# Depthwise convolution in token pairs through DRAM scratch, x loads on the scalar queue, and the gate of group B multiplied in another layout

## What is computed

```python
h = rmsnorm(x, norm_g) * (1.0 + scale[:, None, :]) + shift[:, None, :]
p = h @ w_in                                              # (B, L, 3584)
a_in, a_b, a_c, a_z, b_v, b_g, b_z = jnp.split(p, SPLITS, axis=-1)
y_a = a_b * dwconv(a_c * a_in, conv_a_w) * jax.nn.silu(a_z)          # 3 taps
u = b_v * jax.nn.sigmoid(b_g)
u = dwconv(u, conv_b_w) + conv_b_b                                   # 31 taps
y_b = jax.nn.silu(head_layernorm(u, ln_g, ln_b)) * jax.nn.silu(b_z)
y = jnp.concatenate([y_a, y_b], axis=-1) @ w_out
return x + gate[:, None, :] * y                           # then rmsnorm(., final_g)
```

## Time and profile before

| what | value |
|---|---|
| time, median of 3 runs | 2488.07 us (2486.75 to 2492.78) |
| the profiled execution's own time | 2490.17 us |
| its span, slowest core | 2488.6 us |
| spans of the 8 cores | 2471.5 to 2488.6 us |
| PE busy | 94% of the span |
| DVE, ACT, POOL busy | 47%, 42%, 21% |
| DMA | 142 GB/s on average |

### The profile page before, as it was taken

How to read it: one execution, slowest core, us unless ns; L and a number is a source line. 1 busy time by engine, 2 the same in 40 slices (tenths; PEclk the granted TensorE clock), 3 DMA queues, 4 the chain that set the end, 5 groups by cost and what they waited for, 6 DMA issues and landing times.

```text
span 2488.6 us, 42355 instructions; the slowest of 8 cores (2471.5 to 2488.6 us)
## 1 busy us (share of the span) xinstructions
PE 2330.9 (94%) x13702; PEld 1028.1 (41%) x13702; DVE 1163.8 (47%) x1859; ACT 1056.7 (42%) x1794; POOL 512.7 (21%) x620
## 2 busy tenths in 40 slices
PE   2899799999999999999999799997999979999797
PEld 0343344444444444444444344443444434444343
DVE  0241654445445544444554445454554554544547
ACT  0224444444544444345444245442454434454334
POOL 5112121122211111222121322122221122221203
PEclk9999899999999999999999899998999989999899
DMA  9944444455444445554444653436553445544444
GB/s 232 201 121 115 143 128 114 128 155 155 122 136 138 128 113 138 155 155 121 138 128 128 181 151 116 144 123 162 155 138 121 143 139 155 154 129 130 144 113 179
DMA packets 283012, 352.63 MB, mean 142 GB/s; under 512 B 152840, under 2 KB 225712, under 8 KB 281776
## 3 DMA queue, kind: packets, MB, share of 16 engines
q1 hardware_dynamic: 275184, 342.59, 48.4%
q0 software_dynamic: 7616, 7.34, 2.2%
HBM read 185.73 MB, written 67.13 MB: 102 GB/s over the span
## 4 chain that ended last, share of the span: by engine, by line
PE 86%; DMA 4%; DVE 3%; SPq 2%; issue 2%; POOL 1%; ACT 0%; DVEq 0%; POOLq 0%; ACTq 0%
PE pb L481 56%; PE pb L668 17%; PE pb L553 8%; DMA xb<-w_out 3%; PE pb L465 2%; PE pb L563 1%; SPq L329 1%; DVE tp L536 1%; PE pb L571 1%; DMA hraw<-xs 1%; POOL w_out_sb L447 1%; DMA yT<-w_ada 1%; SPq L292 0%; DVE tp L533 0%; DVE yT L539 0%
## 5 line engine op out<-in xcount | busy, mean ns | idle before, releaser
L481 PE MATMUL pb<-hT,w_in_sb 128*128 128x512 bf16 x6944 | 1507.2, 380 | 2.2 <-DVE hT L454 2.2
L481 PEld LDWEIGHTS pb<-hT,w_in_sb 128*128 128x128 bf16 x6944 | 680.1, 98 | 824.2 <-issue 7.2
L668 PE MATMUL pb<-w_out_sb,yT 128*128 128x512 bf16 x2048 | 460.6, 381 | 5.5 <-POOL yT L591 3.4
L553 PE MATMUL pb<-X,WC 128*32 128x512 bf16 x4096 | 248.5, 390 | 77.1 <-DVE ga L521 77.1
L668 PEld LDWEIGHTS pb<-w_out_sb,yT 128*128 128x128 bf16 x2048 | 199.6, 98 | 247.1 <-issue 19.0
L631 POOL TENSOR_TENSOR rsE<-msE,mhalf 128x1 f32<-128x1 f32 x128 | 70.2, 548 | 1111.5 <-DVE msE L629 1109.2
L513 DVE TENSOR_TENSOR t<-pb,tp 128x512 bf16<-128x512 f32 x128 | 88.9, 694 | 350.3 <-ACT xs L312 322.9
L519 ACT ACTIVATE tp<-pb 128x512 f32<-128x512 f32 x128 | 76.2, 597 | 412.1 <-DVE tp L536 142.7
L492 DVE SCALAR_TENSOR_TENSOR u<-tp,pb 128x512 bf16<-128x512 f32 x128 | 88.4, 691 | 279.5 <-PE pb L481 260.8
L581 DVE SCALAR_TENSOR_TENSOR pb<-pb,cbs,tp 128x512 f32<-128x512 f32 x128 | 96.8, 756 | 257.4 <-PE pb L571 193.8
L490 ACT ACTIVATE tp<-pb 128x512 f32<-128x512 f32 x128 | 76.1, 597 | 329.6 <-PE pb L481 272.1
(11 more groups left out here) (82 smaller groups left out, 1280.9 us busy)
## 6 DMA issues: line engine op xcount, KB each, us to landing
xb<-x SPq DMA_DIRECT2D x252, 512.0 KB, 6.7
X<-u SPq DMA_DIRECT2D x512, 135.0 KB, 2.9
y<-xb SPq DMA_DIRECT2D x124, 512.0 KB, 3.0
xb<-w_out SPq DMA_DIRECT2D x40, 512.0 KB, 8.2
w_in_sb<-w_in POOLq DMA_DIRECT2D x28, 256.0 KB, 22.1
yT<-w_ada SPq DMA_DIRECT2D x6, 1024.0 KB, 10.1
w_out_sb<-w_ada SPq DMA_DIRECT2D x6, 1024.0 KB, 14.8
xb<-gate_scratch SPq DMA_DIRECT2D x5, 512.0 KB, 6.4
```

The costliest lines, as they stand in the source:

```text
L481: T.op("tensor", lambda e, bank=bank, kc=kc: e.matmul(bank[:], lhsT=w_in_sb[:, kc, col0:col0 + 128], rhs=hT[:, kc, :], start=(kc == 0), st ...
L553: T.op("tensor", lambda e, q=q, g=g: e.matmul(bank[32 * g:32 * g + 32, :], lhsT=WC[:, j, g, q, :], rhs=X[:, j, g, 4 * q:4 * q + NT], start ...
L668: T.op("tensor", lambda e, bank=bank, kc=kc, sub=sub, h=h: e.matmul(bank[:], lhsT=yT[:, kc, sub * 128:(sub + 1) * 128], rhs=w_out_sb[:, kc ...
```

## The change

1. **Convolution in token pairs.** A tile's 512 columns are now its 256 odd tokens and then its 256 even tokens (`rows`). A partition of `X` is one of 8 shifts and one of 16 channels. A weight of 32 columns holds 16 channels for the even and the odd output, and one matmul covers 8 input tokens for 256 pairs. `NQ` falls from 8 to 4 and the groups of channels double: still 128 matmuls a tile, each 256 columns wide. The convolution's output has the parity of the token in the partition and both 64-channel halves side by side in the columns, so the norm's vectors (`cbs`, `lng`, `lnb`) differ between halves and several ACT and DVE steps are cut in two.
2. **X through DRAM.** `x_out` writes `u` to `u_scratch` (8 transfers, 544-byte runs), `x_in` reads it back (8 transfers of 16 partitions, 17 KB runs).
3. **The gate in the convolution's layout.** `g_out` and `g_in` bring `gb` through `g_scratch` into that layout, POOL multiplies there, `y_out` and `y_in` bring the product back into `yT`: 10 transfers a tile.
4. **Queues and places.** `a_load` and `d_loads` start on ACT's queue. `a_load` comes after `glu`, `a_square` moves from `t1_group` to `b2_b`, `a_scale` and `a_transpose` to behind `b2_b`, `d_loads` into `b2_a`. The halo copies go from POOL to DVE. All the `ln_*` steps run as hooks of `stage_d`, none between the `conv_b`.
5. **Fold.** `fold_gate` loads its first pieces during `glu`, uses `hraw` and one x buffer as staging, and does all 8 products on POOL.
6. **Start and end.** Tiles 0 and 1 are transposed by PE (`a_modulate`, i < 2) in place of the DMA; the last `stage_d` does the first four of its 8 accumulation steps for all 8 halves first.

```diff
@@ constants
-NQ = 8
-UW = NT + 32
-XW = NT + 4 * (NQ - 1)
+NQ = 4
+HN = NT // 2
+NG = 32
+PAD = 8
+UW = HN + 2 * PAD
+XN = NG * UW - 4
@@ a_load
-                T.dma("sync", lambda e, xbuf=xbuf, r=row0 + sub * 128: e.dma_start(out=xbuf[:], in_=x_d[r:r + 128, :]),
+                T.dma(eng, lambda e, xbuf=xbuf, sub=sub: e.dma_start(out=xbuf[:], in_=rows(x_d, i, sub)),
@@ fold_gate (new)
+            for kc in range(3):
+                load(kc)
+
+            def finish():
+                for kc in range(8):
+                    buf, keys = stg[kc % 3]
+                    T.op("gpsimd", lambda e, buf=buf, kc=kc: e.tensor_tensor(out=w_out_sb[:, kc, :], in0=buf, in1=gate_bc[:], op=ALU.mult),
+                         reads=keys + [gkey], writes=[("w_out", kc)])
+                    if kc + 3 < 8:
+                        load(kc + 3)
...
@@ transfers
-            fns = [lambda e, g=g, k4=k4: e.dma_start(out=X[32 * k4:32 * k4 + 32, :, g, :], in_=u[32 * g:32 * g + 32, :, k4:k4 + XW])
-                   for g in range(4) for k4 in range(4)]
-            T.dma_batch("sync", fns, [("u", slot)], ["X"], "xfill")
+        def x_out(i):
...
+            T.dma_batch("sync", [lambda e, h=h, j=j: e.dma_start(out=dst[h, j], in_=u_sb[i % 2][:, j, h, :]) for h in range(2) for j in range(4)],
+                        [("u", i % 2)], [("ud", i % 2)], "st_u")
...
+            T.dma_batch("sync", [lambda e, w=w: e.dma_start(out=Xf[16 * w:16 * w + 16, 0:XN], in_=ud[i % 2, w % 2, :, (w + 1) // 2:(w + 1) // 2 + XN])
+                                 for w in range(8)], [("ud", i % 2)], ["X"], "xfill")
@@ conv_b
-                        bank[32 * g:32 * g + 32, :], lhsT=WC[:, j, g, q, :], rhs=X[:, j, g, 4 * q:4 * q + NT],
+                            bank[32 * g:32 * g + 32, hh * HN:(hh + 1) * HN], lhsT=WC[:, G * NQ + q].rearrange("p c t -> p (c t)"),
+                            rhs=X[:, G, 4 * q:4 * q + HN], start=(hh == 0 and q == 0), stop=(hh == 1 and q == NQ - 1), tile_position=(0, 32 * g)),
@@ ln_out
-            T.op("gpsimd", lambda e: e.tensor_tensor(out=yT[:, 4 + j, :], in0=r[:], in1=gb[:, j, :], op=ALU.mult),
+            T.op("gpsimd", lambda e: e.tensor_tensor(out=yV[:, j, :], in0=r[:], in1=gbV[:, j, :], op=ALU.mult),
@@ conv_phase
+            cs = [conv_b(j) for j in range(4)]
...
+            return {0: norm((ln_center, 0), (ln_center, 1)),
+                    1: norm((ln_center, 2), (ln_var, 0), (ln_rstd, 0)),
+                    2: norm((ln_center, 3), (ln_var, 1), (ln_rstd, 1)),
+                    3: norm((ln_var, 2), (ln_rstd, 2)),
+                    4: norm((ln_var, 3), (ln_rstd, 3))}, (k, cs)
@@ main loop, behind glu
+            if 1 <= i < ntiles:
+                x_out(i - 1)
+            if left is not None:
+                y_out(i - 2)
+            if 1 <= i < ntiles:
+                x_in(i - 1)
+            if left is not None:
+                y_in(i - 2)
+            left = None
+            if 1 <= i <= ntiles:
+                g_in(i - 1)
+            if 1 <= i < ntiles - 1:
+                a_load(i + 1)
+            if 2 <= i and tile_first[i - 2]:
+                fold()
```

More of the change, by code:

```diff
@@ L539, in conv_a @@
[L539 to L547 removed]
+            out, okey = TP.next()
@@ L661, in stage_d, with half @@
             yT = yT2[i % 2]
-            row0 = i * NT
+            def half(sub, h, kcs, bk=None):
+                bank, bkey = bk or PB.next(pin=kcs[-1] != 7)
+                for kc in kcs:
+                    T.op("tensor", lambda e, kc=kc: e.matmul(
+                        bank[:], lhsT=yT[:, kc, sub * 128:(sub + 1) * 128], rhs=w_out_sb[:, kc, h * NT:(h + 1) * NT],
+                        start=(kc == 0), stop=(kc == 7)),
+                        reads=[("yT", i % 2, kc), ("w_out", kc)], writes=[bkey], signal=(kc == kcs[-1]))
+                return bank, bkey
+            first = [half(n // 2, n % 2, (0, 1, 2, 3)) for n in range(8)] if i == ntiles - 1 else None
             for sub in range(4):
@@ L665, in stage_d @@
                 for h in range(2):
-                    bank, bkey = PB.next()
-                    for kc in range(8):
-                        T.op("tensor", lambda e, bank=bank, kc=kc, sub=sub, h=h: e.matmul(
-                            bank[:], lhsT=yT[:, kc, sub * 128:(sub + 1) * 128], rhs=w_out_sb[:, kc, h * NT:(h + 1) * NT],
-                            start=(kc == 0), stop=(kc == 7)),
-                            reads=[("yT", i % 2, kc), ("w_out", kc)], writes=[bkey], signal=(kc == 7))
+                    bank, bkey = half(sub, h, (0, 1, 2, 3, 4, 5, 6, 7)) if first is None else half(sub, h, (4, 5, 6, 7), first[sub * 2 + h])
                     T.op("vector", lambda e, bank=bank, xbuf=xbuf, h=h: e.tensor_tensor(
```

367 lines of the change are left out of this document (202 added, 165 removed).

## The result

The changed kernel takes 2952.4 us (median of 4 runs) where the kernel before takes 2490.4 beside it: 1.184 times as long, 95% interval 1.180 to 1.188. The forecast was 2300. In some runs of several kernels a die had a lower clock; all ratios, and the times of the experiments (medians), leave those runs out, and the kernel before is then at 2488 to 2490 in every series.

What follows compares the result with a forecast made beforehand. The prediction took PE, busy 94% of the span, to bound the kernel. From 2490.2 us, convolution -121, fold -59, start -14, end -4 and cut steps +9 gave 2301, or 2300 us against the median; range 2250 to 2385.

Steps and rivals of the forecast that it cites:

- Costed at nothing, with their cover: Middle iteration: X and product through DRAM, ACT's issues, squares, scaling, transposes and DMA traffic all hidden, at no cost.
- Rival (c): Transposes start 14 us later, run beside d_loads on another queue and make PE wait; at worst 2660 us; chance 0.07.
- the lag: Output projection: ACT and DVE hold PE back 0.3 us a tile in 30 tiles, +9 us.
- X and the DMA sum: Middle iteration: X lands in 2.9 to 8 us; 2.6 MB more traffic takes some 9 us; no cost to PE.
- The convolution: 128 matmuls a tile at 256 columns instead of 512 save 3.8 us a tile, -121 us over 32 tiles.
- Rival (a): Convolution does not shrink, as weight loads or issue hold a matmul group at its present time: 2415 us, chance 0.06.
- Steps cut in two: Halved ACT and DVE steps, dense at the output projection, cost 0.3 us in 30 tiles, +9 us.
- rival (b): Another engine, ACT or DVE, paces the output projection: at 2 us a tile 2350 us, chance 0.12.
- The fold: Five iterations with a fold: their extra 17.8 us falls to 6 (bounds 0 and 12), -59 us.
- The start: Tile 0 transposed by PE, first projection near 50 instead of 69.8: -14 us (bounds 0 and -20).
- The end: Last projection does half its work before the second halves of yT arrive through DRAM: -4 us.

Runs made afterwards that it cites:

- the best version: Changed kernel with transposes unchained, X on partitions 8 apart, g store behind transposes, squares earlier, fold loads freed and earlier, d_loads on SP behind transposes: 2392.3 us.
- the early squares: The best version with squares, scales and transposes put back at the changed kernel's own late places: 2393.2 us, ratio 0.962.
- the g store's new place: Changed kernel with g_out issued behind the four transposes in place of ahead of them: 2968.0 us, ratio 1.193.
- experiment 18: Changed kernel with transposes unchained, X on partitions 8 apart, d_loads on SP behind transposes, fold loads freed and at iteration's head; g store and squares unmoved: 2373.8 us.
- the first three: Single edits to the changed kernel: transposes unchained, 2784.2 us; X on partitions 8 apart, 2752 us; g store behind the transposes, 2968.0 us.

## Why the prediction was wrong

**The step that failed** is in "Costed at nothing, with their cover": *"Squares at 30 to 37, scaling to 44.4, last transpose landed near 49, `hT` at 52 while DVE's first sum is due at 54"*. Its first half held: the squares stand at 30 to 36 and the scaling is done at 43.3. But the first transpose is issued at 47.0, the last lands near 71 and `hT` is done at 74. Rival (c) named this wait, and its rule comes close: a landing at 71 in place of 54 is 17 us a tile, and the middle iteration is 17.9 us above the 68.0 of the forecast (these hold the slow matmuls after the wait and the lag too, so the fit is partly luck). But I gave it 0.07. Three parts of the step were wrong, each priced by taking its repair back:

- *The transposes as four independent ones.* The change's own line `writes=[("hraw", sub), ("hrawf", 0), ("hrawf", 1)]` stands in the diff. I read it as a wait for the fold and did not carry it through the rule of the helper that a later writer waits for an earlier one. So four landings stand in series, 22.3 us of SP for 5.6. The chain's price with all else repaired is 177 us.
- *X and the DMA sum.* I put X at "2.9 to 8 us" and all new traffic at "some 9 us", by the rate of all transfers. Sixteen neighbouring partitions get 128 GB/s: 17.5 us of all engines for X alone. X itself is not what PE waits for most (63.4 us, 20 times in the whole span); it holds up what is behind it on the queue: the g transfers, which land in 18.3 and 18.8 us, and the transposes. Its price is 214 us. The bound from both sides was taken from the wrong rows: `X<-u` of before writes 32 neighbouring partitions at a time, 1080 bytes in each, at 74 ns a packet in the packet records, so it did not bound a form with 16 from above.
- *`d_loads` on another queue.* This I had in rival (c), with 22.6 us for a transpose that runs beside loads, and set it aside because "x loads of one tile are 2 MB". Its price is 121 us.

Taken alone from the best version the three sum to 512 us, and with the fold (80) and the early squares (1) to 593. The way from the changed kernel to the best version is 560 us in all, so the prices nearly add up; some 20 of the difference is what the g store's new place costs, which the best version has too.

**The convolution: right.** -3.8 us a tile was forecast. 128 matmuls take 3.61 us (3.7 forecast), and with the five norm matmuls that moved, 1.08 us, that is 4.69 for 8.55: -3.86. Rival (a) fell. 3.61 / 128 is 28 ns from one narrow matmul to the next, half of the 56 ns before. The 62 ns that the Trainium skill gives for matmuls decoded in microcode (TensorE: Matmul & The Clock Gate, section "Wait — 56ns, not 53.3ns?") do not agree with this trace either.

**Steps cut in two: the right place, the size wrong.** I took 0.3 us a tile; in the best version the iteration is 69.1 and not 71.48 - 3.86 = 67.6, so it is 1.5. In the iteration shown 1.11 of it is the wait for DVE at the last sums, a small form of rival (b).

**The fold: the wrong sign.** I put what is left of its 17.8 us at 6, with 12 as the upper bound. Four of the five in the changed kernel have 22 to 26 over its middle iterations, the first has 15: five folds cost 112 us over the middle where they had cost 93, and 30 was forecast. SP's and POOL's rows of one fold iteration, and PE's:

```profile
1588.50 12.87 SPq L451 DMA_DIRECT2D hraw<-w_out  x2
...
1639.53 2.98 SPq L451 DMA_DIRECT2D hraw<-w_out  x2
```

```profile
1637.11 2.34 POOL L460 TENSOR_TENSOR w_out_sb<-hraw,xb 128x1024 bf16<-128x1024 f32 x1 [26.81 <-DMA hraw<-w_out]
```

```profile
1632.38 5.15 PE L628 MATMUL pb<-X,WC 128*32 128x256 bf16 x128 [9.45 <-DMA X<-u_scratch]
```

SP stands 12.9 us for the first two loads, since the second waits for the landing of the first, again by a shared key; X is 9.45 us late for PE; loads four to six stand behind X, y and g, and POOL waits 26.8 us for them. I had counted POOL's products and not the queue in front of its loads. Freed, the fold costs 8.5 to 14 us, in the best version: still more than my 6.

**The start: right,** -17.8 for -14, with the second projection at 107.9 (108 forecast). **The end: the wrong sign,** +29.6 for -4. PE stands for the second halves of `yT` on their way through DRAM:

```profile
2882.68 1.86 PE L744 MATMUL pb<-w_out_sb,yT 128*128 128x512 bf16 x4 [12.85 <-DMA yT<-y_scratch]
...
2920.60 9.56 PE L744 MATMUL pb<-w_out_sb,yT 128*128 128x512 bf16 x32 [8.79 <-DMA yT<-y_scratch]
```

I had set the first halves' work against one such trip; there are two, and the first is not covered. The best version has them too, +22.1 us.

For the best version the terms are: start and first two iterations -15.8, middle iterations -55.7, folds -49.6, end +22.1, in all some -99 of span (2389.7 for 2488.6). The forecast of 2300 is not reached even so, nor by experiment 18 (2373.8). In the best version's profiled execution (2391.2) the lag keeps 32 x 1.2 = 38 us, the folds 5 x 5.0 = 25 (11.0 on average where 6 was taken) and the end 26.

**Left open.** The hole of 3.42 us in the convolution has no releaser in the trace. In the packet records a fetch of instructions (16 KB, a transfer too) begins 2.5 us before it ends, in a stretch in which the DMA engines are busy all the time. The same holds for all eight such holes of over 1.5 us before a matmul of the convolution in the changed kernel: each ends 2.3 to 2.7 us after a fetch began. So PE most likely waits there for its instructions, 24.9 us in 12 holes over the whole span; no run tried it. Nor was the end tried.

## What to carry to other kernels

When a change sends data through DRAM, write down the queue that issues it as one line in time, with everything behind it, and read every `writes=` of the diff as a wait: a key that two transfers share puts their landings in series, and that costs nothing in a middle iteration of one kernel and 177 us in another kernel. For a transfer that goes to few partitions, ask which partitions before asking how many bytes. And a repair is to be priced by taking it back from the version where all else works: one by one in the changed kernel, the first three gave -168, -200 and +16, and two that were not among them, the queue of `d_loads` and the fold, decided the sign.
